# Projections of v and r dealt out between the steps of a gated linear attention

## What is computed

```
p = h @ w_in
q, k, v, r, gl = split(p)            # 512, 512, 1024, 1024, 16 columns
log_a = log_sigmoid(gl @ w_g2 + b_g2) / 16
# 4 heads, DK = 128, DV = 256, blocks of 16 tokens
bcum = cumsum(a); qd = q * exp(bcum); kd = k * exp(-bcum)
o = qd @ S + tril(qd @ kd.T) @ v
S = S * exp(blast) + (k * exp(blast - bcum)).T @ v
o = rmsnorm_per_head(o) * g_onorm * silu(r)
x = x + o @ w_out
```

## Time and profile before

| | |
|---|---|
| time, median of three runs | 1588.61 us (1588.29 to 1604.35) |
| span of the profiled execution | 1586.5 us |
| instructions | 26255 |
| TensorE busy | 1514.0 us, 95% |
| weight loads busy | 1464.7 us, 92% |
| VectorE, ScalarE, GpSimd busy | 62%, 35%, 12% |
| mean granted clock of TensorE | 0.979 |

### The profile page before, as it was taken

One profiled execution on the slowest core, in us unless ns is written; L12 is line 12 of the kernel. 1 busy time (PEld: TensorE's weight loads), 2 busy tenths in 40 slices (PEclk: granted clock), 3 DMA queues, 4 the chain that ended last, 5 costly groups with the idle time before them and its releaser, 6 DMA issues.

```text
span 1586.5 us, 26255 instructions
## 1 busy us (share of the span) xinstructions
PE 1514.0 (95%) x10223; PEld 1464.7 (92%) x10223; DVE 982.9 (62%) x1746; ACT 556.6 (35%) x992; POOL 188.9 (12%) x208
## 2 busy tenths in 40 slices
PE   5999987899999999999998999999999999999996
PEld 5999975799999999999998987799999999999996
DVE  6343259735866666666676748724866666666665
ACT  4231344433432323223234337723432333332322
POOL 4000143112100000000004000012100000000000
PEclk9999989899999999999999989999999999999999
DMA  6321311252222222211202510013222222122102
GB/s 216 114 75 59 106 53 60 74 187 90 80 80 79 79 79 79 79 64 68 79 27 57 159 62 2 1 39 107 80 80 79 79 79 72 60 79 79 53 1 90
DMA packets 103636, 122.57 MB, mean 77 GB/s; under 512 B 12210, under 2 KB 96120, under 8 KB 103304
## 3 DMA queue, kind: packets, MB, share of 16 engines
q1 hardware_dynamic: 103576, 121.76, 23.6%
HBM read 109.89 MB, written 11.95 MB: 77 GB/s over the span
## 4 chain that ended last, share of the span: by engine, by line
PE 88%; DVE 8%; ACT 1%; issue 1%; POOL 0%; DMA 0%; SPq 0%; DVEq 0%; ACTq 0%
PE ps L345 52%; PE ps L524 18%; PE ps L370 8%; PE ps L1002 2%; DVE x_lo L434 2%; PE ps L542 1%; PE ps L987 1%; PE ps L356 1%; PE ps L1731 1%; PE ps L967 1%; DVE w_lo L332 1%; DVE masked_scores L1871 0%; DVE scores L1874 0%; DVE x_res L488 0%; PE ps L1013 0%
## 5 line engine op out<-in xcount | busy, mean ns | idle before, releaser
L345 PE MATMUL ps<-x_hi,w_hi 128*128 128x320 f32 x1904 | 435.8, 310 | 12.4 <-DVE x_lo L434 6.9
L345 PE MATMUL ps<-x_lo,w_hi 128*128 128x320 f32 x1904 | 434.4, 309 | 0.0
L345 PE MATMUL ps<-x_hi,w_lo 128*128 128x320 f32 x1904 | 434.0, 309 | 0.0
L345 PEld LDWEIGHTS ps<-x_hi,w_hi 128*128 128x128 f32 x1904 | 318.4, 188 | 14.7 <-DVE w_lo L332 5.3
L345 PEld LDWEIGHTS ps<-x_hi,w_lo 128*128 128x128 f32 x1904 | 318.8, 188 | 0.0
L345 PEld LDWEIGHTS ps<-x_lo,w_hi 128*128 128x128 f32 x1904 | 318.7, 188 | 0.0
L325 ACT ACTIVATE w_hi<-w_raw 128x1024 fp32r<-128x1024 f32 x139 | 146.1, 1058 | 459.8 <-PE ps L345 393.0
L488 DVE TENSOR_TENSOR x_res<-x_res,ps 128x640 f32<-128x640 f32 x192 | 153.7, 817 | 133.6 <-PE ps L345 65.5
L332 DVE TENSOR_TENSOR w_lo<-w_raw,w_hi 128x1024 fp32r<-128x1024 f32 x139 | 171.4, 1239 | 48.7 <-ACT w_hi L325 41.2
L802 POOL TENSOR_TENSOR tail_cols<-up_rows,ones 128x4 f32 (+1 forms) x44 | 51.2, 1164 | 827.5 <-DVE up_rows L608 773.2
L524 PE MATMUL ps<-gated_lo,d_hi 128*128 128x320 f32 x640 | 145.8, 309 | 0.0
(11 more groups left out here) (231 smaller groups left out, 1930.3 us busy)
## 6 DMA issues: line engine op xcount, KB each, us to landing
w_raw<-in_ffn_w_up_dram SPq DMA_DIRECT2D x44, 1024.0 KB, 5.2
d_raw<-in_ffn_w_down_dram SPq DMA_DIRECT2D x22, 1024.0 KB, 5.0
w_raw<-in_gla_w_in_dram SPq DMA_DIRECT2D x12, 1024.0 KB, 5.3
w_raw<-in_gla_w_out_dram SPq DMA_DIRECT2D x4, 1024.0 KB, 9.6
seq_states<-in_state_gla_dram SPq DMA_DIRECT2D x4, 1024.0 KB, 5.4
out_dram<-seq_states SPq DMA_DIRECT2D x4, 1024.0 KB, 4.4
w_raw<-in_att_w_q_dram SPq DMA_DIRECT2D x4, 1024.0 KB, 6.1
w_raw<-in_att_w_o_dram SPq DMA_DIRECT2D x4, 1024.0 KB, 5.1
```

The costliest lines, as they stand in the source:

```text
L345: mm = pe.matmul(PS[:, 2 * (u0 % 4) + f, 0:HALF], w[:, n0 % 4, k, :], x[:, k, f * HALF:(f + 1) * HALF], start=(k == 0 and a == 0), stop=(k ...
```

## The change

The columns of v and r are taken by head: r of head 0, v of head 0, r of head 1, and so on, one piece of 256 columns each. One token tile of one such piece is a group of 24 matmuls. Ten groups (r and v of head 0) stand ahead of the steps. The other thirty are dealt to the steps: in each step the first group of its share stands between `scores` and `outputs`, the rest behind `outputs`. The groups have two PSUM banks; scores, transposes and outputs have one each, the states three. `outputs` of a step comes before `scores` of the next. ScalarE takes r out as a plain copy and applies Silu to a whole head at once (`gate_r`). v is kept for two heads. The level operands share one buffer for queries and keys (odd blocks hold the one, even blocks the other), so the exponential of the levels is one or two instructions per head, and the zero fills on GpSimd fall away. Loads of weights are mixed with the loads and stores of the states on SyncE's queue. The work for the next head is moved by about a step in each list.

```diff
+        def group_end(n):
+            if n < 0:
+                return 2 * TT
+            return min(2 * TT + (26 * (n + 1) + 7) // 15, GROUPS) if n < STEPS - TT else min(22 + n, GROUPS)
...
+        SC_B, TR_B, O_B, ST_B, VR_B = 2, 3, 5, (4, 6, 7), (0, 1)
...
+            pe.wait_ge(free, U_Z + 4)
+            for m in range(2 * TT):
+                vr_group(pe, m)
             gla_pe(pe)
...
+            for m in range(3):
+                vr_evict(v, m)
+            v.wait_ge(s_mn, H + 2)
             v.tensor_tensor(LA[:, :, :], LA[:, :, :], AB[:, :, :], ALU.subtract).then_inc(s_la, 1)
+            vr_evict(v, 3)
...
             gla_sums(v, 0)
+            vr_evict(v, 4)
+            gla_levels(v, 0)
+            for n in range(2):
+                rest_tile(v, T_VR + 4 + n)
             gla_operands(v, 0)
+            vr_evict(v, TT)
             gla_queries(v, 0)
+            vr_evict(v, TT + 1)
+            gla_level_operands(v, 0)
+            for m in range(TT + 2, 2 * TT):
+                vr_evict(v, m)
+            for n in range(2):
+                rest_tile(v, T_VR + 6 + n)
             gla_dve(v)
...
+            act.wait_ge(vr_full, TT)
+            for n in range(2):
+                round_tile(act, T_VR + 4 + n)
             gla_exps(act, 0)
+            gla_level_exps(act, 0)
+            gate_r(act, 0)
+            act.wait_ge(vr_full, 2 * TT)
+            for n in range(2):
+                round_tile(act, T_VR + 6 + n)
             gla_act(act)
...
+        def group(m):
+            q = m // TT
+            return q // 2, q % 2, GO[m % TT]
...
+        def gate_r(act, h):
+            act.wait_ge(r_free, TT * (h + 1))
+            r = RS[:, :, DV * h:DV * h + DV]
+            act.activation(r, r, ACT.Silu).then_inc(gated_r, 1)
...
+        def vr_group(pe, m):
+            n0 = T_VR + 2 * (m // TT)
+            t = GO[m % TT]
+            pe.wait_ge(lo_done, n0 + 2)
+            if m >= 2:
+                h, is_v, _ = group(m - 2)
+                pe.wait_ge(v_free if is_v else r_free, TT * h + (m - 2) % TT + 1)
+            for k in range(KT):
+                for a, (x, w) in enumerate(((XH, WH), (XH, WL), (XL, WH))):
+                    mm = pe.matmul(PS[:, VR_B[m % 2], 0:DV], x[:, k, 128 * t:128 * t + 128],
+                                   w[:, n0 % 4:n0 % 4 + 2, k, :],
+                                   start=(k == 0 and a == 0), stop=(k == KT - 1 and a == 2))
+            mm.then_inc(vr_full, 1)
...
+        def vr_evict(e, m):
+            h, is_v, t = group(m)
+            e.wait_ge(vr_full, m + 1)
+            i_, r = PS[:, VR_B[m % 2], 0:DV], RT[:, t:t + 1]
+            if is_v:
+                e.tensor_scalar(V[:, t, DV * (h % 2):DV * (h % 2) + DV], i_, r, None, ALU.mult).then_inc(v_free, 1)
+            elif h == 0:
+                e.tensor_scalar(RS[:, t, 0:DV], i_, r, None, ALU.mult).then_inc(r_free, 1)
+            else:
+                e.activation(RS[:, t, DV * h:DV * h + DV], i_, ACT.Copy, scale=r).then_inc(r_free, 1)
...
+            for n in range(STEPS):
+                scores(n)
+                for m in before_out(n):
+                    vr_group(pe, m)
+                outputs(n)
+                for m in behind_out(n):
+                    vr_group(pe, m)
+        def fill(n):
+            return range(group_end(n - 1), group_end(n))
...
+        def before_out(n):
+            return fill(n)[:1]
...
+        def behind_out(n):
+            return fill(n)[1:]
@@ gla_exps @@
+            if h == 1:
+                act.wait_ge(prep, 2)
+                act.wait_ge(prepp, 1)
+                act.wait_ge(prepl, 1)
+                act.wait_ge(preplp, 1)
@@ gla_dve @@
+            for n in range(STEPS):
+                h, j = n // TT, n % TT
+                mask(n)
+                for m in before_out(n):
+                    if group(m)[1]:
+                        vr_evict(v, m)
+                after(n)
+                for m in behind_out(n):
+                    if group(m)[1]:
+                        vr_evict(v, m)
+                for m in fill(n):
+                    if m % TT == TT - 1:
+                        for x in range(2):
+                            rest_tile(v, T_VR + 2 * (m // TT) + 4 + x)
+                if j == 1 and h + 1 < H:
                     gla_sums(v, h + 1)
                     gla_levels(v, h + 1)
+                if j == 2 and h:
+                    head_inverse(v, h - 1)
+                if j == 3 and h + 1 < H:
                     gla_operands(v, h + 1)
+                    gla_queries(v, h + 1)
+                if j == 4 and h + 1 < H:
                     gla_level_operands(v, h + 1)
@@ gla_act @@
+            for n in range(STEPS):
+                h, j = n // TT, n % TT
+                keys(n)
+                for m in before_out(n):
+                    if not group(m)[1]:
+                        vr_evict(act, m)
+                out_squares(n)
+                for m in behind_out(n):
+                    if not group(m)[1]:
+                        vr_evict(act, m)
+                for m in fill(n):
+                    if m % TT == TT - 1:
+                        act.wait_ge(vr_full, m + 1)
+                        for x in range(2):
+                            round_tile(act, T_VR + 2 * (m // TT) + 4 + x)
+                        if m // TT % 2 == 0:
+                            gate_r(act, m // TT // 2)
+                if j == 1 and h:
+                    head_root(act, h - 1)
+                if j == 2 and h + 1 < H:
+                    gla_exps(act, h + 1)
+                    gla_level_exps(act, h + 1)
+                if j == 3 and h:
+                    act.wait_ge(rt_h, 2 * h)
+                    act.wait_ge(og, TT * h)
                     for g in range(TT):
+                        mm = scale_head(act, h - 1, g)
                     mm.then_inc(ogh, 1)
```

More of the change, by code:

```diff
@@ L90, in build @@
         RT = sb("rstd_rows", [128, TT])
[L91 removed]
+        ss_area = area(4 * T)
+        SS = at("sum_sq", [128, T], F32, ss_area)
         NVEC = 54
@@ L255, in build @@
         s_table = sem("s_table")
+        vr_full = sem("vr_full")
+        r_free = sem("r_free")
+        v_free = sem("v_free")
+        gated_r = sem("gated_r")
         s_out = sem("s_out")
@@ L285, in build @@
         pieces += [(w_in, H * DK + 256 * n) for n in range(2)] + [(w_in, 256 * n) for n in range(2)]
-        pieces += [(w_in, 2 * H * DK + 256 * n) for n in range(8)]
+        pieces += [(w_in, 2 * H * DK + H * DV * (1 - n % 2) + DV * (n // 2)) for n in range(2 * H)]
         pieces += [(A["gla_w_out"][0], 256 * n) for n in range(4)]
@@ L1339, in piece, with state_in, state_out, last_state_out @@
                     .then_inc(s_raw[p % 2], 16)
[L1341 to L1348, removed]
+            def state_in(h):
+                if h:
                     sp.wait_ge(s_sout, 16 * h)
                 sp.dma_start(S0[:, :, :], A["state_gla"][0, :, h].rearrange("s p d -> p s d")).then_inc(s_s0, 16)
[L1351 to L1356, removed]
+            def state_out(h):
+                sp.wait_ge(st_done, 8 * h + 4)
+                sp.dma_start(O["gla_s"][0, :, h].rearrange("s p d -> p s d"), S0[:, :, :]).then_inc(s_sout, 16)
+            def last_state_out(h):
+                sp.wait_ge(st_done, 8 * h + 8)
+                sp.dma_start(O["gla_p"][0, 0, h], ST[:, :]).then_inc(s_pout, 16)
+            p_vr = T_VR // 2
+            for p in range(2, p_vr + 4):
+                piece(p)
+            sp.wait_ge(full, U_Z + 4)
+            state_in(0)
+            piece(p_vr + 4)
+            piece(p_vr + 5)
+            for h in range(H):
+                state_out(h)
+                if h + 1 < H:
+                    state_in(h + 1)
+                if h < 3:
+                    piece(p_vr + 6 + 2 * h)
+                last_state_out(h)
+                if h < 2:
+                    piece(p_vr + 7 + 2 * h)
             sp.wait_ge(att, STEPS)
             sp.dma_start(X[:, :, :], XSP).then_inc(s_xback, 16)
-            for p in range(T_WO // 2 + 2, T_WO // 2 + 4):
-                piece(p)
+            piece(T_WO // 2 + 3)
             sp.wait_ge(full, U_WO)
@@ L1731, in outputs @@
                             mm = pe.matmul(PS[:, b, DV * e:DV * e + DV], KTK[r, 2 * (n % 2) + e, :],
-                                           V[r, g, DV * h:DV * h + DV], start=True, stop=True,
+                                           V[r, g, DV * s:DV * s + DV], start=True, stop=True,
                                            tile_position=(32 * x, 0))
                     mm.then_inc(st_full, 1)
-            scores(0)
-            outputs(0)
-            for n in range(1, STEPS + 1):
-                if n < STEPS:
-                    scores(n)
-                if n > 1:
-                    outputs(n - 1)
+            for n in range(STEPS):
[5 more added lines that the diff above has]
+                    vr_group(pe, m)
         def span(ap, l, odd):
```

(2 more changed lines are left out.)

190 lines of the change are left out of this document (60 added, 130 removed).

## The result

The changed kernel takes 1607.56 us (median of 12 runs, 1605.38 to 1610.75). Against the kernel before the ratio is 1.0115, 95% interval 1.0092 to 1.0139: some 18 us slower. I had forecast 1594, 0.3% slower, as likeliest, and a fall of the clock, 1606, as the rival.

The account below looks back on a forecast made before the run. TensorE was taken as the bound: groups 115.2, heads 62.8, start 7.8 and waits 32 made 217.8 us against 216.8; with 1 for hand-overs and 3 for the clock, +5 us, 1588.6 becomes 1594, range 1568 to 1612.

Parts of the forecast that it names:

- a fall of the clock: Slower rival: TensorE's rests of 3 us and more each bring 1.2 GHz, 15 us in place of 3; 1606, chance 0.18.
- the clock's term of the sum: Half clock after TensorE's rests of 4.9 and 6.8 us in the steps: 1.5 us each, 3 us; ends 0 and 18.
- the hand-overs: Some forty more switches between fp32 products and groups in the twenty steps, 0.03 us each: 1 us.
- The signs: Prediction wrong if the last step ends before 298 us, output products hardly wait, or the steps' granted clock stays under 0.85.
- The waits: TensorE waiting in the steps for longer VectorE or ScalarE lists: 32 us together, the worst 6.8 us in step 12.
- The two small waits of the start: Group 9 waits 1.2 us; two weight tiles rounded behind it delay the first mask by 0.6 us.
- The one-group cover of the mask: A 2.88 us group between scores and outputs covers the 1.75 us masking if VectorE is free when scores arrive.
- Order, not load: Waits in the steps come from the order of VectorE's and ScalarE's work, as their busy time stays far below TensorE's.
- My faster rival: VectorE and ScalarE lists in the steps hide better: 16 us of waits instead of 32, 1575; chance 0.25.
- Full serial: Rival: a group between scores and outputs only lengthens its step; 223.8 us, 1596; shares chance 0.53 with the forecast.
- Weight loads and GpSimd at nothing: Twelve GpSimd zero fills removed and a new order of weight loads, each issued at least four steps early: no effect.
- The tail at no change: The part of the kernel from 313.5 us on, behind the last step, stays unchanged.

Follow-up runs that it names:

- e1: Changed kernel plus discarded matmuls in TensorE's waits at the start and in steps 2, 3, 9, 12 and 19: 1596.39 us, ratio 1.0074 to the kernel before.
- e2: Changed kernel with VectorE's next-head preparation and weight remainders moved behind the following step's mask: 1580.03 us, ratio 0.9962 to the kernel before.
- e4: Changed kernel with all groups of a step behind its outputs, none between scores and outputs: 1658.0 us, ratio 1.0472 to the kernel before.
- e7: e2 with ScalarE's gate, exponentials and head scaling also moved behind the following step's key copy, a repeat run: 1574.98 us, ratio 0.9926 to the kernel before.
- e6: e7 with group 0 waiting only for the first gate eviction, and evictions of groups 5 to 7 put earlier: 1567.93 us, ratio 0.9880 to the kernel before.
- e8: Changed kernel plus 50 discarded matmuls in the mask wait of step 12 alone: 1605.08 us, ratio 1.0109 to the kernel before.

## Why the prediction was wrong

**The step that failed** is the clock's term of the sum: "1.5 us each, 3 us", two drops. There were nine: seven behind rests of TensorE (99 and 123 us at the start, 164, 177, 239, 269 and 327 us behind the waits of steps 2, 3, 9, 12 and 19) and two in first steps (146 and 252 us). Summed over stretches of 1 us, 46.1 us were at 1.2 GHz, with TensorE busy in 37.0 of them; so the clock cost 16 to 18.5 us, which is the upper end that I had given for the term, 18. The balance of the stretch closes: 237.1 us less 40.2 of waits (24.4 + 5.4 + 6.6 + 3.8) is 196.9 us of work, as the row has it, where my sum had 217.8 less 42.4 (7.8 + 32 + 2.6), that is 175.4. Of the 21.5 us between, 16 to 18.5 are the clock. The rest, 3 to 5 us, is the size of the hand-overs, for which I had 1: in the 30 places where a group stands behind other work, its second matmul starts 0.20 us or more behind its first in place of 0.12, some 4 us in all. The mechanism was in the text as the slower rival, with a chance of 0.18 and 1606 us; so the mistake was to give it to the rival and the small number to the forecast. e1 shows it apart from the waits.

**Why I undersized it.** The kernel before is at 1.2 GHz for 0.15 x 2 x 100.8 = 30 us of its steps too, and I took this for a cost that it bears and the new one loses. I also read today's steps wrong. I set 60 us of TensorE at full clock against 100.8 and called the 40 us between rest. TensorE is busy for 81.66 us of them, and its waits in the steps sum to 19.5 us, so only half of the 40 was rest that groups could fill. Much of the other half is the low clock: TensorE is busy in 26.5 of the 30 us, which makes 12 to 13 us by the same estimate. Nor is that hidden under VectorE's list throughout:

```profile
300.00:304.00 4.00, 4.00 (x16) 3.16 (x15) 1.76 (x5) 0.28 (x1) 0.00 (x0) 0.53 0.00 0
304.00:308.00 4.00, 4.00 (x17) 3.46 (x17) 3.05 (x6) 0.94 (x4) 0.00 (x0) 0.62 0.00 0
```

In these 8 us of the kernel before, 6.8 of them at 1.2 GHz, TensorE never rests and VectorE is busy for 4.8. So both kernels pay for a low clock, the changed one for 10 us more of busy time (37.0 against 26.5), some 5 us. I ran no kernel before with its clock held, so what it pays stays an estimate. The Trainium skill's section "Why this matters for your kernels" (of "TensorE: Matmul & The Clock Gate") speaks against bursts with gaps between them; e1 and the seven drops behind rests agree, the two in first steps had no such gap, and by that rule, which I had put down as the rival, 1606 was the time to forecast.

**What made it slower than the kernel before** is not the clock in the main: TensorE's rest doubled, from 20.1 to 40.2 us, at the same busy time. e1, which gives back most of the clock, stays above the kernel before; e2, which takes away most of the rest, comes out below it. The 5 us more that the clock costs, and the hand-overs, don't show in the busy time, so something else in it became less; what, these rows don't say.

**The signs.** The first step began at 135.4 us (131 to 133 forecast), the last state product ended at 332.8 (310 to 325), the clock over the steps was 0.91, and the largest waits stood where I had named them. Of the three signs by which I wanted to know a wrong prediction none came: I had set none for a late end.

**The waits** were right in place and size: 29.8 us against 32 in the steps, 6.6 against 6.0 in the two large ones of the start (6.45 counted from the end of the gate products). The two small waits of the start (1.2 and 0.6) don't appear among the large ones. **The one-group cover of the mask** was right: only steps with a long list waited, and e4 shows what the cover is worth. **Order, not load** was right: e2 wins 27.5 us by order alone. My faster rival was thus a fact about another kernel: with lists that hide, the change comes out at 1580 (e2), and at 1575 (e7), which is its 1575. That the two agree is in part luck, as e7 still has the low clock that this rival left out. **Full serial** (1596) gave nearly the time of the forecast and was not told apart from it; e4 excludes it, since a kernel without cover is 50 us worse. **Weight loads and GpSimd at nothing:** no wait of TensorE names them. **The tail at no change** was short by little: its transposes take 5.88 us in place of 3.68, as the drop behind step 19 reaches them.

## What to carry to other kernels

When work is dealt out into an engine's pauses, list for each pause what the other engines must finish in it, in their written order; put the work that is needed late behind the hand-over that is needed now (here 27.5 us for the order of one list). Price a rest of TensorE twice: as the rest, and as the work at half clock that follows it. And before you call a gap between a sum at full clock and the measured time rest, compare it with the waits and with the granted clock: here 40 us of such a gap held 19.5 us of waits.

## What the runs showed of the hardware

Discarded matmuls in the rests of TensorE raised its granted clock from 0.90 to 0.98 and gave 11 us. 128x256 matmuls of the groups started 0.12 us apart at 2.4 GHz and 0.21 us apart at 1.2 GHz.

Drops also came behind the first steps of heads 0 and 2 (146 and 252 us in the changed kernel), where TensorE rested only 0.9 us at a time between short products with 32 rows, and not behind those of heads 1 and 3. Which first steps it is changes with the kernel: in e6 and e7 they are those of heads 0, 1 and 3 (144, 188 and 273 us in e6), in the profile of e8 none; in e6 they are three of the four drops left. Each has the same rest of 0.9 us; why some bring a drop and others don't, these runs don't settle.
